# The last expert's down product by halves of the output columns, with the first half's scatter and squares beside the second half

## The reference

```
def moe_swiglu(x, w_router, w_gate, w_up, w_down):
    logits = (x @ w_router).astype(jnp.float32)
    top_val, top_idx = lax.top_k(logits, TOP_K_EXPERTS)
    gate = jax.nn.softmax(top_val, axis=-1)
    combine = ...                      # (B, T, 8): the gate of an expert for a token, or 0
    out = jnp.zeros_like(x)
    for e in range(N_EXPERTS):
        out = out + combine[..., e:e + 1] * swiglu(x, w_gate[e], w_up[e], w_down[e])
    return out
...
            x = x + moe_swiglu(rms_norm(x, p['norm_ffn_odd'][i]), ...)
    y = rms_norm(x, p['norm_final'])
```

## Time and profile before

| what | us |
|---|---|
| median of three executions | 1423.42 |
| lowest, highest of them | 1417.24, 1429.50 |
| the profiled execution | 1419.75 |
| its span, first to last instruction | 1417.9 |
| TensorE (PE) busy in the span | 1363.7 |
| VectorE (DVE) busy | 613.4 |
| ScalarE (ACT) busy | 235.8 |
| data moved, MB, and mean rate, GB/s | 377.66, 266 |

### The profile page before, as it was taken

One profiled execution on the slowest core, in us unless ns is written; L12 is line 12 of the kernel. 1 busy time (PEld: TensorE's weight loads), 2 busy tenths in 40 slices (PEclk: granted clock), 3 DMA queues, 4 the chain that ended last, 5 costly groups with the idle time before them and its releaser, 6 DMA issues.

```text
span 1417.9 us, 39974 instructions
## 1 busy us (share of the span) xinstructions
PE 1363.7 (96%) x18028; PEld 937.6 (66%) x18028; DVE 613.4 (43%) x1252; ACT 235.8 (17%) x547; POOL 224.2 (16%) x271
## 2 busy tenths in 40 slices
PE   7899999999999999888899999999999999999996
PEld 5667899999997778786535546455464554646453
DVE  3599378777648477735323112120131202212153
ACT  3144121111016222413200000101000010000102
POOL 5148002221002442242030000000000000000100
PEclk9999999999999999989999999999999999999998
DMA  9454063432443400127869999999999999999992
GB/s 376 182 190 119 1 239 120 179 139 100 164 178 106 121 16 3 62 73 296 326 265 393 404 414 404 414 414 401 414 402 415 402 413 413 398 408 412 405 384 86
DMA packets 86020, 377.66 MB, mean 266 GB/s; under 512 B 11967, under 2 KB 12959, under 8 KB 85594
## 3 DMA queue, kind: packets, MB, share of 16 engines
q1 hardware_dynamic: 77712, 353.77, 63.7%
q0 software_dynamic: 4832, 17.17, 3.3%
q10 hardware_dynamic: 3306, 4.17, 0.8%
HBM read 367.15 MB, written 7.91 MB: 265 GB/s over the span
## 4 chain that ended last, share of the span: by engine, by line
PE 88%; DVE 8%; ACT 2%; issue 1%; DMA 0%; SPq 0%; DVEq 0%
PE bk L1771 32%; PE bk L1788 16%; PE bk L1076 10%; PE bk L819 10%; PE bk L1686 2%; PE bk L1024 2%; PE bk L1361 1%; DVE left L2398 1%; DVE tops L2396 1%; PE bk L1282 1%; PE bk L1243 1%; PE bk L1235 1%; PE bk L1227 1%; PE bk L1217 1%; PE bk L1209 1%
## 5 line engine op out<-in xcount | busy, mean ns | idle before, releaser
L1771 PE MATMUL bk<-part,xe 128*32 128x352 f32 x6144 | 460.0, 460 | 2.4 <-DVE xe L2961 2.4
L1771 PEld LDWEIGHTS bk<-part,xe 128*32 128x32 f32 x6144 | 194.8, 110 | 263.1 <-issue 258.3
L1788 PE MATMUL bk<-part,hidT 128*32 128x256 f32 x4224 | 232.0, 379 | 0.0
L1788 PEld LDWEIGHTS bk<-part,hidT 128*32 128x32 f32 x4224 | 167.6, 110 | 62.2 <-issue 2.6
L3029 DVE TENSOR_TENSOR hp<-sg,bk 128x352 f32<-128x352 f32 x48 | 37.3, 776 | 353.5 <-PE bk L1771 353.4
L819 PE MATMUL bk<-mx,ring 128*128 128x288 f32 x384 | 96.2, 409 | 0.0
L819 PE MATMUL bk<-xg,ring 128*128 128x288 f32 x336 | 86.0, 414 | 8.5 <-DMA ring<-in_weights 8.3
L3055 DVE COPY ye<-bk 32x256 f32<-32x256 f32 x48 | 20.3, 422 | 150.9 <-PE bk L1788 150.3
L819 PEld LDWEIGHTS bk<-mx,ring 128*128 128x128 f32 x384 | 72.0, 190 | 20.4 <-issue 0.9
L819 PEld LDWEIGHTS bk<-xg,ring 128*128 128x128 f32 x336 | 63.9, 193 | 26.7 <-issue 8.9
L3300 POOL TENSOR_TENSOR free_rows<-row_ss 128x1 f32 x7 | 5.4, 770 | 472.6 <-DVE xe L2970 447.1
(11 more groups left out here) (596 smaller groups left out, 1648.7 us busy)
## 6 DMA issues: line engine op xcount, KB each, us to landing
part<-in_moe_gate SPq DMA_DIRECT2D x128, 704.0 KB, 16.7
part<-in_moe_up SPq DMA_DIRECT2D x128, 704.0 KB, 16.6
part<-in_moe_down SPq DMA_DIRECT2D x128, 704.0 KB, 14.5
ring<-in_weights SPq DMA_DIRECT2D x121, 512.0 KB, 5.9
ro<-in_weights SPq DMA_DIRECT2D x8, 512.0 KB, 7.9
expert_rows<-ye ACTq DMA_DIRECT2D x7, 384.0 KB, 7.0
Ss<-in_states SPq DMA_DIRECT2D x1, 2048.0 KB, 7.7
out_wkv_sample<-Ss SPq DMA_DIRECT2D x8, 256.0 KB, 2.7
```

Source lines behind the costliest of these rows:

```text
L1771: last = mm(banks[g][32 * c:32 * c + 32, 0:FQ], xe[:, k, 32 * g:32 * g + 32], parts[PART_OF[ph]][:, FH * k + FQ * c:FH * k + FQ * c + FQ], ...
L1788: last = mm(down_bk[g // 2][32 * q:32 * q + 32, 256 * (g % 2):256 * (g % 2) + 256], hidT[:, half, g, 32 * m:32 * m + 32], parts[PART_OF[ph ...
```

## The change

The down product of the last expert is done by halves of the output columns. A half is 128 of the 256 columns of each quarter. TensorE's list for it is now: hidden half 0 for column half 0; the transposes of `give`; hidden half 1 for column half 0; hidden half 0 for column half 1; three scatters of column half 0; hidden half 1 for column half 1; and behind the loop three scatters of column half 1. Column half 1 is summed in PSUM banks 0 and 1 instead of 6 and 7. Each product has 128 columns, and there are twice as many.

ScalarE and VectorE copy `ye` in two lots of 32 x 128. Beside the second half VectorE adds the first half's scatter to `acc` and multiplies it with the gain into a new tile `acc_g`, and ScalarE takes its squares. After the end of the product the final norm squares half the columns, takes the root with the first half's sum as bias, and the first half of `y_out` is made by ScalarE from `acc_g` (`first_columns`), the second by VectorE. SP and ScalarE wait for both halves before they issue an output.

```diff
-    SCATTER = ((0, 0), (0, 1), (1, 0), (1, 1), (2, 0), (2, 1))
+    SCATTER = ((0, 0), (1, 0), (2, 0), (0, 1), (1, 1), (2, 1))
...
+    columns = lambda x, half: x.rearrange("p (q h d) -> p h q d", q=4, h=2)[:, half]
...
+        banks = (bk[6:8], bk[0:2])[half]
+        for q in quarters:
+            for g in range(3):
+                last = copied(ye[32 * g:32 * g + 32, 256 * q + P * half:256 * q + P * half + P],
+                              banks[g // 2][32 * q:32 * q + 32, 256 * (g % 2):256 * (g % 2) + P])
...
+        def narrow_columns(blk, ph, half, out_half):
+
+            banks = (down_bk, gate_bk)[out_half]
+            for m in range(NM):
+                if out_half == 0:
+                    for i in range((D * m) // FH + (m > 0), (D * m + D - 1) // FH + 1):
+                        piece(blk, LAST, ph, i)
+                for g in range(3):
+                    if m == 0 and out_half == 0:
+                        pe.wait_ge(hid_ok, blk * (6 * NE) + PAIRS + 6 * LAST + 3 * half + g + 1)
+                    for q in range(4):
+                        at = D * m + 256 * q + P * out_half
+                        last = mm(banks[g // 2][32 * q:32 * q + 32, 256 * (g % 2):256 * (g % 2) + P],
+                                  hidT[:, half, g, 32 * m:32 * m + 32], parts[PART_OF[ph]][:, at:at + P],
+                                  start=half == 0 and m == 0 and g != 1, stop=half == 1 and m == NM - 1,
+                                  skip_group_check=True)
...
+            narrow_columns(blk, 4, 0, 0)
+            pe.wait_ge(silu_ok, blk * (6 * NE) + PAIRS + 6 * e + 6)
+            pe.wait_ge(pick_ok, blk + 2)
+            for i, (t0, tn) in enumerate(TILES):
+                last = nc.tensor.transpose(gate_bk[2][0:CAP, t0:t0 + tn], give[0:tn, i], C["ident"][0:tn, 0:tn])
+            last.then_inc(gt_mm, 1)
+            narrow_columns(blk, 5, 1, 0).then_inc(down_mm, 1)
+            narrow_columns(blk, 4, 0, 1)
+            for g in range(3):
+                scatter(blk, g)
+            narrow_columns(blk, 5, 1, 1).then_inc(down_mm, 1)
...
-            for g in range(6):
+            for g in range(3, 6):
                 scatter(blk, g)
...
+        def root_mean(i):
+
+            tn = TILES[i][1]
             act.wait_ge(sc_ok, n_blocks * 6 + DONE_AT[i])
-            nc.scalar.activation(y_out[0:tn, i], acc[0:tn, i], ACT.Square, accum_out=ssf[0:tn, i:i + 1]).then_inc(sq_ok, 1)
+            nc.scalar.activation(columns(y_out[0:tn, i], 1), columns(acc[0:tn, i], 1), ACT.Square,
+                                 accum_out=pos[0:tn, i, 1:2]).then_inc(sq_ok, 1)
+            act.wait_ge(sq_ok, 2 * KC + 7 + i)
+            nc.scalar.activation(ssf[0:tn, i:i + 1], pos[0:tn, i, 1:2], ACT.Sqrt, bias=ssf[0:tn, i:i + 1],
+                                 scale=1.0 / D).then_inc(sd_ok, 1)
...
+        root_mean(0)
+        root_mean(1)
+        first_columns(0)
+        root_mean(2)
+        first_columns(1)
+        first_columns(2)
+        act.wait_ge(lo_ok, LO_N + 2)
         act.wait_ge(fin_ok, 2)
         act.dma_start(O["y_prompt"][0, P:2 * P, :], y_out[:, 1]).then_inc(out_done, 16)
```

More of the change, by code:

```diff
@@ L448, in build @@
     got = sbt("got", [P, 2, D], at=starts["xT"])
+    acc_g = sbt("acc_g", [P, 3, 4, P], at=starts["xT"])
     token_no = sbt("token_no", [P, 3, 32])
@@ L1751, in scatter @@
                 pe.wait_ge(sc_ok, blk * 6 + 6 + g - 2)
+            of_half = ye[:].rearrange("p (q h d) -> p h q d", q=4, h=2)[:, half]
             t0, tn = TILES[i]
@@ L1755, in scatter @@
                 last = mm(up_bk[g % 3][at:at + 32, :], giveT[:, t0 + 32 * q:t0 + 32 * q + 32],
-                          ye[:, 512 * half:512 * half + 512], start=True, stop=True)
+                          of_half, start=True, stop=True)
             last.then_inc(sc_mm, 1)
@@ L1795, in narrow @@
             last.then_inc(down_mm, 1)
+        def narrow_columns(blk, ph, half, out_half):
[13 more added lines that the diff above has]
+                                  skip_group_check=True)
+                if m < NM - 1 and out_half == 1:
+                    last.then_inc(piece_use, 1)
+            return last
         def expert(blk, e):
@@ L1826, in expert @@
                 pe.wait_ge(row_ok, blk * 3 + (SEL_OK + 1))
[L1827 to L1834, removed]
+            if e < LAST:
+                narrow(blk, e, 4, 0)
+                narrow(blk, e, 5, 1)
+                return
+            narrow_columns(blk, 4, 0, 0)
[9 more added lines that the diff above has]
+            narrow_columns(blk, 5, 1, 1).then_inc(down_mm, 1)
         pe.wait_ge(blocks_ok, 1)
@@ L3012, in rows_in, with add_rows @@
                                        ALU.mult, ALU.add).then_inc(spot_then_rows, 1)
[L3014 to L3022, removed]
+        def add_rows(blk, g):
+            i, half = SCATTER[g]
+            tn = TILES[i][1]
+            dve.wait_ge(sc_mm, blk * 6 + g + 1)
+            a = columns(acc[0:tn, i], half)
+            at = 32 * half * (i == 2)
+            return V.tensor_tensor(a, up_bk[g % 3][at:at + tn, :].rearrange("p (q d) -> p q d", q=4), a,
+                                   ALU.add).then_inc(sc_ok, 1)
         def hidden(blk, e, half):
@@ L3050, in expert @@
                 dve.wait_ge(rows_out, blk * (16 * LAST) + 16 * e)
+            if e == LAST:
+                dve.wait_ge(spot_then_rows, blk * 7 + 7)
+                for half in range(2):
+                    dve.wait_ge(down_mm, blk * (2 * NE) + DOWN_N + 2 * e + 1 + half)
+                    columns_out(V.tensor_copy, (1, 3), half).then_inc((ye_ok, scaled_mix_then_ye)[half], 1)
+                    for g in range(3 * half, 3 * half + 3):
+                        if g == 3:
+                            dve.wait_ge(sc_mm, blk * 6 + g + 1)
+                            V.tensor_scalar(ssf[:], pos[:, :, 0], 1.0 / D, EPS, ALU.mult, ALU.add)
+                        add_rows(blk, g)
+                    if half == 0:
+                        dve.wait_ge(sc_ok, blk * 6 + 6 + 3)
+                        for i, (t0, tn) in enumerate(TILES):
+                            V.tensor_tensor(acc_g[0:tn, i], columns(acc[0:tn, i], 0), columns(gain_f[0:tn], 0), ALU.mult)
+                return
             dve.wait_ge(down_mm, blk * (2 * NE) + DOWN_N + 2 * e + 2)
@@ L3111, in _ @@
         columns_in()
+        dve.wait_ge(rt_in, 32)
         with dve.Fori(0, n_blocks) as blk:
```

40 lines of the change are left out of this document (28 added, 12 removed).

## The result

The changed kernel takes 1429.66 us (median of 6 runs, 1428.18 to 1431.82) against 1421.80 us for the kernel before (6 runs). The medians are 7.9 us apart. The ratio is 1.0049, 95% interval 1.0026 to 1.0071, which is 7.0 us (3.7 to 10.1): the changed kernel is slower. Its profiled execution took 1431.82 us with a span of 1430.0.

What follows compares the result with a forecast made beforehand. TensorE, 96% busy, was taken to bound the kernel, with the last down weights landing only 2 to 3 us ahead. Later product end +11.0, tail -5.6 and clock +1.3 gave +6.7 us, stated as 1429 us, range 1418 to 1438.

Steps and rivals of the forecast that it cites:

- The landings bind in the new order: Last expert's down product: TensorE reaches the second weight buffer early and waits about 9 us for pieces to land.
- From the first product to the last landing: Last expert's first two down passes: start at 1371.2, waits about 3.5 us apart, last piece landing at about 1393.1.
- the slack of 2 to 3 us: Last expert's down phases before the change: each pair of weight pieces lands 2 to 3 us before TensorE asks for it.
- the share 0.50: End of the weight stream: 206 GB/s at half the engines' share, read as a backlog on half of the DMA engines.
- Behind the last landing: After 1393.1: 1.94 us of steps, a pass (7.1), three scatters (2.1), a pass (7.1), 0.3 for the last product, all unhindered.
- Splitting costs TensorE next to nothing: Last expert's down product: 128-column records at 27.0 ns each, two passes 14.25 us against 14.45 for one old phase.
- Rival A: Last expert's down product: weights land in time, TensorE runs through, -3.6 us, about 1419; chance 0.13.
- Rival C: Last expert's down product: issue of small products binds at 28.9 ns or more, +7.7 us; chance 0.01.
- The clock term: Last expert's down product: waiting lowers TensorE's clock for a stretch; +1.3 us taken, bounds 0 and 3.4.
- Rival B: Down passes at half clock: +12.3 us, about 1435, chance 0.13; sign: product end past 1416 with PEclk 0.5 before it.
- The tail: From product end to span end: copies, scatters, additions, norm and output take 11.7 us, 5.6 shorter than before.
- rival D: Tail does not shrink because ScalarE's extra products and waits are dearer: up to +5.6 us more, about 1434; chance 0.05.

Runs made afterwards that it cites:

- by_tokens: Kernel before, with the last expert's down product in four passes split by token group, 256-column products kept and no more of them: ratio 1.0075.
- by_tokens_no_wait: Kernel before, four passes by token group, last expert's down products reading the up buffer without waiting for down pieces: ratio 0.9997.
- before_no_wait: Kernel before, old order, last expert's down products reading the up buffer without waiting for down pieces: ratio 1.0005.
- small_mid: Kernel before, with two 128-column products in place of each 256-column one in both down phases of expert 3 only: ratio 1.0104.
- no_stream: Changed kernel, last expert's down products reading the up buffer without waits, and its 16 down pieces not transferred at all: ratio 0.9990.
- no_wait: Changed kernel, last expert's down products reading the up buffer without waiting for down pieces, which are still transferred: ratio 1.0047.
- small_products: Kernel before, old order, each down product of the last expert done as two of 128 columns one behind the other: ratio 1.0050.
- group_last: Kernel before, last five steps of the last down phase by token group, so copies of groups 0 and 1 run beside group 2's products: ratio 0.9988.

## Why the prediction was right, and where a step of it was not

The forecast was 1429 and the range 1418 to 1438; measured is 1429.66. The mechanism that it went by, waiting for landings in the new order, is there. That the number came within 1 us is in part luck: the steps were off by 3.2 us in sum, one of them hid a second limit that is just as tight, and the forecast was set from a mean of four executions that vary by 12 us. Step by step:

- **The landings bind in the new order.** Right, and shown in isolation (by_tokens, by_tokens_no_wait, before_no_wait). Predicted were about 9 us of waiting; 10.0 and 9.5 were found. Five gaps were named and all five are there; two more, of 1.6 us at m = 2 of the first pass and 0.9 at m = 0 of the second, were not foreseen.
- **From the first product to the last landing** 21.9 us were expected; 24.4 passed (1373.2 to 1397.6). The spacing of 3.5 us held; the last piece came 3.9 behind the one before it, and the whole row of landings stood later against TensorE than in the one trace that I had. There SP issued the last piece 2.9 us after TensorE's first down product; in the other traces (small_mid and no_stream apart) it did so 3.3 to 4.4 us after it, 4.4 in the changed kernel. The one trace was the most favourable of all, and with it the slack of 2 to 3 us. The reading of the share 0.50 as a backlog on half of the DMA engines fits a count in the trace of before: 16 packets of weights were under way at a time over 1373 to 1379 us, and 8 (7 to 9) over 1381 to 1389.
- **Behind the last landing** 18.6 us were expected, 19.1 found, with no gap. The three scatters took 2.7 instead of 2.1.
- **Splitting costs TensorE next to nothing.** Wrong. 27.0 ns per record is right inside a burst, and TensorE's own pace does not show that the instructions come only every 6.2 us beside the stream. The earlier trace rows stand in a stretch where next to nothing else was in transfer, 14 GB/s, and 128 records are just one block:

```profile
178.90:182.60 3.70, 3.70 (x130) 3.50 (x130) 2.10 (x4) 0.28 (x1) 0.00 (x0) 1.00 0.06 14
```

  In the changed kernel the mistake stayed hidden: 128 records per 6.2 us are 72 per 3.5 us, and 72 per 3.5 us is also what the landings allow. The two limits coincide, so their costs don't add up, and lifting one alone (no_wait) brings little.
- **Rival A's price** rested on that step and falls with it. With the weights there in time, I had 3.6 us faster; no_wait measured 1.0047, some 6.7 us slower. Rival C, too, was priced as time per product and held 1 in 100 for something that costs 7 us alone (small_products, 1.0050).
- **The clock term**, +1.3 us, was nothing. TensorE was busy 14.38 of 24.40 us while it waited, a share of 0.59 like that in the earlier trace rows, and its granted clock stayed at 1.00. Rival B has fallen: the product did end past 1416, the first half of its sign, but without a low clock before it. The share does not settle it, since at 0.59 the clock fell in the earlier trace rows and stayed here. What the Trainium skill describes in the section quoted there, every tile at the low clock, does not show in this trace, with waits of 0.9 to 1.9 us.
- **The tail** was to be 11.7 us and is 13.2. The copies were right, and the first scatter started at +2.0 (1418.78 - 1416.80), but it was done at +3.5 instead of +2.9. ScalarE's final product took 0.72 instead of 0.60, the root 0.29 instead of 0.20, the additions ended at +7.2 instead of +6.3, and the output took 3.0 instead of 2.4. The tail shrinks by 4.1 us in the pair of profiles (17.3 to 13.2) and by 3.2 where the clock is full for all of the scatters or nearly so (15.6 to the 12.4 of no_stream); 5.6 was forecast. So rival D came true for 1.5 of its up to 5.6 us.

Against the sum of +6.7: landings +2.5, behind them +0.5, tail +1.5, clock -1.3 give +9.9 for the pair of profiles, and 2.2 more lie before the stage begins, in which nothing was changed. The medians differ by 7.9, and the interval of the ratio reaches from 3.7 to 10.1 us.

What stays open: why an instruction block takes 6.2 us beside the stream. A packet is 1.0 to 1.1 us long and starts 3.5 to 4.7 us after the burst before it began; whether it is asked for so late or stands behind the weights until then, no run shows. Whether weights in other packet sizes would change it was not tried.

## What to carry to other kernels

Before work is split or reordered to gain cover, ask what feeds it at the new pace, and ask it twice: when does each piece of data land against the step that reads it, and when does each block of instructions land. An engine that shows no wait may be only 2 us ahead of its data, and may take 7 us for a block of instructions of which the next comes after 6.2. Cover is best taken where the stream has ended, and in pieces that make no more instructions and no earlier demand, as group_last does; what it can gain is then the tail that it really shortens, here 1.3 us in the trace.

## What the runs showed of the hardware that was not expected

- TensorE stopped for 2.2 to 3.3 us after each 128 records of products with their weight loads while weights came at 322 to 405 GB/s (small_mid, 1049 to 1068 us) or 185 to 278 (small_products, 1380 to 1392), and not at all with no weights in transfer (no_stream); behind the end of the stream the gaps of no_wait were 0.32 us. The bursts start 6.2 us apart (once 7.0) in small_mid, 5.9 and 6.2 in small_products, and each gap ends 1.3 to 1.6 us after a packet of the instruction queue has landed. Products of 256 columns, 128 records of which last 7 us, never showed it (before, before_no_wait, by_tokens_no_wait).
- The pieces of weights land in two rows: in the kernel before the even pieces of the last expert's down phases landed 9.3 to 12.9 us after their issue, the odd ones 19.2 to 22.1, and the stream's end runs at half the engines' share (0.50 over 1381 to 1383 us, 0.46 over 1386 to 1392 us of small_products). In the kernel before only 8 packets of weights were under way at a time over 1381 to 1389 us, after 16 over 1373 to 1379. It looks as if each piece had one half of the 16 engines; the trace does not name a packet's engine, and why is open. So each pair under one semaphore was as late as its odd piece.
- The granted clock stayed at 1.00 through 24 us in which TensorE was busy for 0.59 of the time with gaps of at most 1.9 us, and through 33 us at 0.56 with gaps of up to 3.3 us in small_mid, behind which it stood at 0.50 for 3.4 us. In rows 7 of the kernel before it fell behind a stretch at 0.59.
